# mLSTM of a two-block kernel on one core: order of the gate, head and log-weight loads, place of the mask, gate and numerator steps, an early exp table

## What is computed

```python
D = b[..., :, None] - b[..., None, :] + ig[..., None, :]      
m_comb = jnp.maximum(jnp.max(D, axis=-1), m_inter)
Dw = jnp.exp(D - m_comb[..., None])
s = jnp.einsum('bhcid,bhcjd->bhcij', qc, kc) * Dw
num = jnp.einsum('bhcij,bhcje->bhcie', s, vc) + ...
den = jnp.sum(s, axis=-1) + ...
h = num / jnp.maximum(jnp.abs(den), jnp.exp(-m_comb))[..., None]
...
h_ml = rmsnorm_2(h_ml, ml_head_norm.reshape(ML_HEADS, ML_V))
h_ml = h_ml * jax.nn.sigmoid(o_ml.astype(jnp.float32)).reshape(B, S, ML_HEADS, ML_V)
```

## Time and profile before

| | |
|---|---|
| median of three runs | 2906.31 us |
| profiled execution | 2903.81 us |
| its span | 2902.1 us, 32962 instructions |
| TensorE matmul / weight load | 2775.1 us (96%) / 2194.5 us (76%) |
| VectorE / ScalarE / GpSimd | 1805.2 (62%) / 1020.4 (35%) / 1275.0 us (44%) |
| chain that ended last | TensorE 78%, VectorE 12%, DMA 3%, issue 3%, ScalarE 2% |

### The profile page before, as it was taken

One profiled execution on the slowest core, in us unless ns is written; L12 is line 12 of the kernel. 1 busy time (PEld: TensorE's weight loads), 2 busy tenths in 40 slices (PEclk: granted clock), 3 DMA queues, 4 the chain that ended last, 5 costly groups with the idle time before them and its releaser, 6 DMA issues.

```text
span 2902.1 us, 32962 instructions
## 1 busy us (share of the span) xinstructions
PE 2775.1 (96%) x12594; PEld 2194.5 (76%) x12594; DVE 1805.2 (62%) x2066; ACT 1020.4 (35%) x1382; POOL 1275.0 (44%) x768
## 2 busy tenths in 40 slices
PE   7999899999998999999998999999898999999997
PEld 5888688877776888887786886666477688878776
DVE  3111354656746666668889667665537766777885
ACT  4000333333224333334443114456435433343443
POOL 2434222223435788883333434002332888833331
PEclk9999999999999999999999999999899999999999
DMA  5222232334342333337531534003333355564443
GB/s 176 96 92 95 96 118 86 128 105 145 128 148 66 95 109 109 102 111 235 170 117 37 197 111 122 1 32 100 87 123 107 103 153 160 174 207 149 160 143 119
DMA packets 336967, 348.91 MB, mean 120 GB/s; under 512 B 18915, under 2 KB 256602, under 8 KB 336822
## 3 DMA queue, kind: packets, MB, share of 16 engines
q1 hardware_dynamic: 327254, 311.30, 34.7%
q10 hardware_dynamic: 9568, 35.66, 3.1%
HBM read 237.53 MB, written 108.34 MB: 119 GB/s over the span
## 4 chain that ended last, share of the span: by engine, by line
PE 78%; DVE 12%; issue 3%; DMA 3%; ACT 2%; POOL 1%; SPq 1%; DVEq 0%; ACTq 0%; POOLq 0%
PE ps L3235 34%; PE ps L528 29%; PE ps L2344 2%; PE ps L2366 2%; DVE op_lo L3312 2%; PE ps L935 1%; PE ps L564 1%; DVE sw_lo L3145 1%; PE ps L2354 1%; PE ps L2684 1%; PE ps L916 1%; PE ps L570 1%; PE ps L869 1%; PE ps L2811 1%; DMA w_raw<-in_w_out 1%
## 5 line engine op out<-in xcount | busy, mean ns | idle before, releaser
L3235 PE MATMUL ps<-op_hi,sw_hi 128*128 128x512 f32 x1769 | 695.0, 393 | 19.7 <-DVE op_lo L3312 8.9
L3235 PE MATMUL ps<-op_lo,sw_hi 128*128 128x512 f32 x1769 | 690.6, 390 | 0.0
L3235 PE MATMUL ps<-op_hi,sw_lo 128*128 128x512 f32 x1769 | 690.4, 390 | 0.0
L497 POOL TENSOR_TENSOR w_hi_t<-w_raw,ones 128x1024 fp32r<-128x1024 f32 x79 | 162.0, 2051 | 694.9 <-PE ps L528 356.8
L3235 PEld LDWEIGHTS ps<-op_hi,sw_hi 128*128 128x128 f32 x1769 | 333.6, 189 | 100.5 <-issue 18.6
L3235 PEld LDWEIGHTS ps<-op_lo,sw_hi 128*128 128x128 f32 x1769 | 333.6, 189 | 69.8 <-issue 1.0
L3235 PEld LDWEIGHTS ps<-op_hi,sw_lo 128*128 128x128 f32 x1769 | 333.5, 189 | 69.8
L651 DVE TENSOR_TENSOR stage<-ps,rstd 128x1024 f32<-128x1024 f32 x62 | 75.7, 1221 | 346.0 <-PE ps L528 327.6
L3135 ACT ACTIVATE sw_hi<-sw_sumNone 128x512 fp32r<-128x512 f32 (+1 forms) x252 | 157.1, 624 | 339.2 <-PE ps L3235 257.1
L528 PE MATMUL ps<-h1hi,w_hi_t 128*128 128x512 f32 x720 | 234.3, 407 | 13.0 <-DVE h1lo L612 9.0
L3145 POOL TENSOR_TENSOR sw_lo<-sw_sumNone,sw_hi 128x512 fp32r<-128x512 f32 x138 | 214.7, 1565 | 39.2 <-ACT sw_hi L3135 39.1
(11 more groups left out here) (435 smaller groups left out, 4935.8 us busy)
## 6 DMA issues: line engine op xcount, KB each, us to landing
op_raw<-hidden SPq DMA_DIRECT2D x42, 1024.0 KB, 8.6
w_raw<-in_w_in SPq DMA_DIRECT2D x60, 512.0 KB, 3.8
sw_raw<-in_w_ffn_in SPq DMA_DIRECT2D x44, 512.0 KB, 5.2
proj<-stage ACTq DMA_DIRECT2D x42, 512.0 KB, 2.6
hidden<-hidden_blocks SPq DMA_DIRECT2D x13, 1536.0 KB, 6.2
acc<-proj SPq DMA_DIRECT2D x36, 512.0 KB, 4.0
hidden<-hidden_blocks SPq DMA_DIRECT2D x14, 1280.0 KB, 5.0
sw_raw<-in_w_up SPq DMA_DIRECT2D x32, 512.0 KB, 8.3
```

Source lines behind the costliest of these rows:

```text
L497: pool.tensor_tensor(h, r, ones[:, 0:1].to_broadcast([P, n]), ALU.mult).then_inc(S["w_hi"], 1)
L3235: mm = pe.matmul(out, w, x[:, k, :], start=(k == 0 and i == 0 and r < 4), stop=(k == n - 1 and i == 2), skip_group_check=r >= 4)
```

## The change

It moves waits and instructions in the lists; one activation of one column is new and nothing is left out. In SyncE's list the wait for the end of attention goes behind row 5; the head loads go behind rows 7 and 14; the gate load of head 0 goes behind row 6 and those of heads 1 to 3 behind the row of their own head's J = 4. On VectorE the mask goes from three steps ahead to two. On ScalarE the numerator is copied first and the copy is squared, after a wait for the copy; the head copies go from steps 9 and 17 to 10 and 18; the sigmoid goes from J = 2 to J = 6. In the attention, an exp of one column is put between the two copies of head 7, and GpSimd's split of the output weight waits for the value product of head 0's last query tile. `small[:, 44:45]` is read by nobody.

```diff
--- before.py
+++ after.py
@@ -2188,7 +2188,7 @@
             for h in range(8):
                 for i in range(2):
                     split_head(pool, h, i)
-            pool.wait_ge(S["q_rope"], 8)
+            pool.wait_ge(S["pv_ready"], 8)
 
         def turned_values(h):
             return PS[3][:, h % 2 * HALF:h % 2 * HALF + HALF]
@@ -2207,6 +2207,8 @@
                     act.wait_ge(S["mq_stored"], 64)
                 act.wait_ge(S["unit_done"], uq.times(1, 1))
                 act.activation(qT[NOPE, h, :], q_bank(h)[NOPE, :], ACT.Copy).then_inc(S["q_copied"], 1)
+                if h == 7:
+                    act.activation(small[:, 44:45], ones[:, 0:1], ACT.Exp)
                 act.wait_ge(S["unit_done"], uk.times(1, 1))
                 act.activation(kT[NOPE, h, :], PS[uk.par][NOPE, :], ACT.Copy)
                 if h:
@@ -2454,15 +2456,14 @@
                 if J == 3 and h < 3:
                     sp.wait_ge(S["mv_t"], h + 1)
                     sp.dma_start(vTm, proj2[(5 + h) * P:(6 + h) * P, :]).then_inc(S["mv_loaded"], 16)
-                if n == 3:
+                if n == 5:
                     sp.wait_ge(S["pv_ready"], 64)
-                    om_sp(sp, 0)
-                    head_load(sp, 2)
-                if n == 12:
-                    sp.wait_ge(S["qk_back"], 64 * 3)
-                    head_load(sp, 3)
-                if J == 7 and h < 3:
-                    om_sp(sp, h + 1)
+                if n in (7, 14):
+                    if n == 14:
+                        sp.wait_ge(S["qk_back"], 64 * 3)
+                    head_load(sp, 2 + n // 14)
+                if n % C == (4 if h else 6):
+                    om_sp(sp, h)
 
         def turned_at(h):
 
@@ -2482,8 +2483,9 @@
         def num_act(act, h):
 
             act.wait_ge(S["ho_ready"], C * (h + 1))
-            act.activation(sqb, PS[2][:, :], ACT.Square).then_inc(S["h_sq"], 1)
             act.activation(hn, PS[2][:, :], ACT.Copy).then_inc(S["num_copied"], 1)
+            act.wait_ge(S["num_copied"], h + 1)
+            act.activation(sqb, hn, ACT.Square).then_inc(S["h_sq"], 1)
 
         def root_act(act, h):
             act.wait_ge(S["h_step"], HS * h + 7)
@@ -2520,10 +2522,10 @@
                     log_weight_act(act, n + 2)
                 if h and J == 0:
                     num_act(act, h - 1)
-                if n in (9, 17):
+                if n in (10, 18):
                     for i in range(2):
-                        head_hi(act, 2 + n // 17, i)
-                if J == 2:
+                        head_hi(act, 2 + n // 18, i)
+                if J == 6:
                     gate_act(act, h)
                 if h and J == 2:
                     root_act(act, h - 1)
@@ -2613,8 +2615,8 @@
                 dve.scalar_tensor_tensor(out=Wt[:, n % 3, s], in0=PS[n % 2][:, s], scalar=0.125,
                                          in1=erow[n % ER][:, s], op0=ALU.mult, op1=ALU.mult)\
                    .then_inc(S["st_w"], 1)
-                if 4 <= n + 3 < NS:
-                    mask_dve(dve, n + 3)
+                if 4 <= n + 2 < NS:
+                    mask_dve(dve, n + 2)
                 if n == 1:
                     mixa_low(dve, 7)
                 if h and J == 0:
```

## The result

| | before | after |
|---|---|---|
| median, same chip, 5 runs each | 2905.49 us (2904.11 to 2907.57) | 2917.21 us (2913.52 to 2919.92) |
| profiled execution, its span | 2903.81, 2902.1 us | 2913.52, 2911.8 us |

After is slower: the ratio is 1.0038, interval 1.0026 to 1.005. The forecast was 2906.3 with a range up to 2915; it is 11 us short, and the median lies above the range.

What follows compares the result with a forecast made beforehand. The prediction took the mLSTM as bound by a relay of latencies, not TensorE's rate, despite TensorE's 96% of the span. mLSTM +1.8 and attention -1.85 summed to 0.0, so the forecast was 2906.3 us, range 2898 to 2915.

Steps and rivals of the forecast that it cites:

- Attention's start: Attention: early exp table load, half clock ending sooner and the moved split, together -1.85 us, between -4.3 and +1.1.
- Head 0, rows 4 and 5: mLSTM head 0: these log-weight rows, issued ahead of the gate and head-2 loads, land sooner; -5.5 us at tile 6.
- the wait at three head ends: Head boundaries: the sigmoid at tile 6 delays the copy the denominator waits for; +2.4, +1.5 and +2.3 us.
- the root behind a later mask: Heads 1 to 3: the later mask's exp, and head copies in two heads, delay the root; +2.9, +2.9, +1.0 us.
- rows 16 and 24: mLSTM: these log-weight rows no longer wait behind the gate load; -3.5 us twice, -7.0.
- end: End of the mLSTM: exp 31 precedes the last high copy and the last sum starts later; +0.6 us.
- The clock: mLSTM: full clock after rows 16 and 24, -3.8 us; new half clock +1.5 at each of two roots and one boundary.
- What would show it: Signs: no mask wait for rows after 2003, TensorE idle 2.3 to 2.5 us before the denominator, VectorE's root waits.
- rival 3: mLSTM: rows 16 and 24 are late anyway, behind head loads or a later sigmoid; 2913.3 us, chance 0.04.
- the split in head 1: Attention near 1840: GpSimd's moved split meets one of VectorE's scales; +1.9 us.
- rival 1: Every boundary and root is followed by half clock until TensorE's next idle; 2914.8 us, slower, chance 0.17.
- rival 4: Table switches: the skill page's drain of 1.38 us beside each load is paid; 2918 us, chance 0.01.

Runs made afterwards that it cites:

- e6_filler: The changed kernel with 20 unread transposes of a constant ahead of each of the first three denominators; 2910.24 us, ratio 1.0015.
- e5: The kernel before with SyncE's new order of loads and nothing else; 2889.58 us, ratio 0.9942.
- e1: The changed kernel with the gate's sigmoid at tile 4 instead of 6; 2901.61 us, ratio 0.9979.
- e2: The changed kernel with the mask three steps ahead again; 2898.05 us, ratio 0.9972.
- e7: e5 with the sigmoid at tile 6 instead of 2; 2896.92 us, ratio 0.9965.
- e8: e5 with the mask two steps ahead instead of three; 2907.88 us, ratio 1.0004.
- e12: The changed kernel with the numerator squared from PSUM first and copied second; 2917.6 us, ratio 1.0035.
- e9: e5 with early exp table, head 0's gate load and sigmoid earlier, other sigmoids behind the root, head 2's load behind row 9; 2885.69 us, ratio 0.9935.

## Why the prediction was wrong

Each step against the shifts in the table above:

| step of the prediction | forecast | in the profile of after |
|---|---|---|
| Attention's start | -1.85 | -1.1 |
| Head 0, rows 4 and 5 | -5.5 | -5.6 |
| the wait at three head ends (`Wt` of tile 6 to denominator) | +6.2 | +8.4 (4.25, 1.66, 2.49) |
| the clock at head ends | -3.8 +1.5 | +2.6 (the rest of +11.0) |
| the root behind a later mask | +2.9 +2.9 +1.0 | +2.7 +2.7 +0.8 |
| the clock behind two roots | +3.0 | +4.7, three roots |
| rows 16 and 24 | -3.5 twice | -3.5 twice |
| end | +0.6 | +2.8 |

The right column adds up to 11.0; 0.9 was won ahead of the change's first instruction and 0.4 behind the mLSTM, which leaves the 9.7 between the spans.

The parts that were read from latencies came out: head 0, the roots and both late rows within 0.7 us together. **The step that failed is "The clock"**: for new stretches of half clock it charged 4.5 us, 1.5 "at a boundary", one of three, and 1.5 on each of two roots. The clock fell at all three boundaries, at all three roots and before the last denominator. At the boundaries the runs show some 6 us in place of 1.5: e6_filler, which keeps the clock at 1.00 there and leaves ScalarE's list as it was, gets them back. At the roots it is 4.7 in place of 3.0. The end is the same miss, +2.8 in place of +0.6: it holds a denominator of 3.73 us and the first matmuls of line 528 behind it. The 3.8 given back behind rows 16 and 24 was sound where nothing else changed: e5 gains 17.1 us where the prediction's terms for the loads, clock with them, were 16.3.

A smaller miss is the wait at the first boundary. From `Wt` of tile 6 to the denominator I had 7.4 us; it is 9.24. The exp of tile 8 starts 1.7 later than I assumed, as row 8 lands behind the four loads of head 2 (VectorE's mask waits 1.57 us, until 2012.05). "What would show it" asked for no such wait after 2003. That is the cause that rival 3 named for row 8; it costs some 2 us and not 7. It also makes the -5.6 at tile 6 in part luck, of where the mark was put: with the mask three ahead (e5) the wait for row 8 falls ahead of that `Wt`, and head 0 gains 3.7.

It also asked for TensorE idle 2.3 to 2.5 us before the denominator; it was 4.18, 3.85 and 3.87. At the second boundary the distance is 7.57, what the prediction had (7.4), and only the idle was misread. Before, TensorE's last scores ahead of the denominator ran at half clock and ended 5.9 us after `Wt` of tile 6, right at the denominator; the prediction kept that end for after. In after they run at full clock and end 3.7 us after it (2050.93), and the faster they end the longer TensorE stands. The last scores, in the timeline of before and then of after:

```profile
2052.51 1.11 PE L2662 MATMUL ps<-q_parts,k_low 64*128 64x384 f32 x2
```

```profile
2050.26 0.67 PE L2664 MATMUL ps<-q_parts,k_low 64*128 64x384 f32 x2
```

So the full clock that came back with row 16 lengthened the very wait in which it was lost again. Over all profiles of this case, TensorE's waits of 2.6 to 4.7 us before one of the first three denominators were all followed by half clock (17), and those of 0.3 to 1.7 us never (12, in e1, e2, e6, e7, e8).

One term of attention was mis-sized as well: the split in head 1 was priced at +1.9 and costs 5.0 in all seven profiles that have it there.

So rival 1 was the right one, "the clock decides upward", 2914.8 at a chance of 0.17: its condition, 0.50 in four places or more, is met with seven. (Before had four already, so that sign alone could not have told them apart; falls at every boundary and root do.) Its point of decision was put at the roots, where VectorE's wait of 4.28 us and TensorE's of 3.80 agree with it; but more of the loss is at the head ends. My argument against it, that idle of 1 to 2 us at full clock is common, spoke of shorter waits than these. What the forecast said of VectorE's wait in line 2584 (2586 in after) was right: 4.28, 4.27 and 2.38 us against "about 4" and "1.5 to 2.5".

Smaller points. The terms of the root add up to 7.0 and not 6.9 us (6.8 was measured), and the least that attention's own terms allow is -5.05, not -4.3. The square-first order was priced at 0.7 and costs nothing (e12). The prediction of one long scale near 1840 was right in kind: split and scale met at 1833, below. The exp table is loaded at 1800.21, in idle time of ScalarE as forecast; TensorE's idle behind it is 0.50 instead of 1.92. Whether it left the chain can't be said, as the chain of after is followed back to 2082.56 only. Timeline of after in attention:

```profile
1805.54 1.45 PE L2346 MATMUL ps<-kT,acc 96*128 96x384 f32 x2 [0.50 <-ACT x L2226]
...
1832.93 2.34 POOL L499 TENSOR_TENSOR w_lo_t<-w_raw,w_hi_t 128x1024 fp32r<-128x1024 f32 x1
...
1833.29 2.20 DVE L2293 TENSOR_SCALAR x<-x,small 128x384 f32<-128x384 f32 x1
```

Head 0 of attention ran 6.1 us sooner, at a clock near 1.00 where it was 0.71; in head 1 this meeting and a stretch of half clock behind it gave 5.0 back. So -1.1 against a forecast of -1.85 is luck twice over: two terms that were both too small, and a good start (the seven profiles average +0.5).

The drain of a table switch (rival 4) doesn't show: in after an activation that waits for nothing else starts 0.01 us behind its 1.28 us load, as at 2013.55 and 2015.92. The Trainium skill (ScalarE: Activation LUTs, What ACT_TABLE_LOAD costs) puts 1.38 us beside it; no run here shows them. Its rule to group activations by table set is not borne out as a count of loads: the mLSTM of after has 14, before and e5 have 12, but e1 has 15 and is faster than both before and after. What cost time in after is where two of them stand, at tile 6 in front of the copy that the denominator waits for.

What stays open: why the start of attention varies by some 4 us between profiles of the same code; how much of e9's gain over e5 is the early exp, which no run has alone; and how the delays at root and head end combine beyond the additive table (the mask alone costs 18.3 in e8, where sigmoid and root stand together, against 6.8 and 3.0 of clock in the forecast). That the clock makes some 6 us at the head ends is shown by e6; at the roots (4.7 us) it is read from durations and was not taken away by a run.

## What to carry to other kernels

In a relay between engines, a step that is moved later in one engine's list pushes everything queued behind it: read the list between the moved wait and the next thing another engine stops for, and count every instruction in it, as the mask moved by one step (18 us) shows. Then ask how long TensorE stands in each new wait and price the matmuls behind a wait of 4 us at half clock, at every place and not at one. A change that bundles a good part with bad ones is worth taking apart: loads alone were 17 us faster, the whole was 9 to 12 slower.

## What the runs showed that was not expected

- The granted clock falls inside the wait. TensorE stopped at 2015.1 and the window 2017 to 2018 shows 0.67, the next 0.50, before a single matmul of the denominator has run. Behind the first root, with an idle stretch of 3.80, the window 2037 to 2038 shows 0.91 and the next 0.50: it fell when TensorE was busy again. In head 3 an idle stretch of 1.90 before 2105.76 was followed by 0.54 and 0.50 from 2106 on, while one of 1.92 before 2045.18 was followed by none: the length of the last idle stretch alone does not decide. How long it stayed down differs: 2018 to 2024 at the first head's end, 3 us at the second.
- Work that nobody reads can pay: 20 transposes of 2.40 us in all, put into a wait of about 4, made the kernel 5 to 8 us faster (e6). Taking the wait away is better: e1 gains 14 to 17.
- A longer wait costs more than its length. In e8 the first root's `Wt` to `Wt` grew by 3.2 us, and the two steps behind it by another 3.1.
- Some of VectorE's small instructions on SBUF stretch to the end of a GpSimd instruction that runs beside them: the scale at 1833.29 of after takes 2.20 us beside one of 2.34, step 8 in e9 1.80 beside one of 1.81. Others don't: the one-column scaling at 1804.51 of before takes 0.15 us inside a GpSimd instruction of 1.90. A wait removed ahead of such an instruction can bring it into one, as in e9, and then gives nothing.
